# Weight slabs of 1 MB instead of 2 MB, and ten slots for gathered pairs instead of eight, in a two-block model kernel

## What is computed

```python
s1 = einsum("thd,hnd->thn", q1, k1)
s2 = einsum("thd,hnd->thn", q2, k2)
...
experts = (e1 * N_KEYS + e2)              # per token: 8 heads x 16 experts = 128
gates = softmax(sv)
hid = gelu(einsum("td,tkd->tk", xi, u_tab[ei]))
out = einsum("tk,tkd->td", gi * hid, v_tab[ei])
```

## Time and profile before

| what | value |
|---|---|
| time, median of 3 runs | 2146.59 us (2145.9 to 2158.28) |
| profiled execution | 2149.26 us |
| its span, as the profile counts it | 2147.5 us |
| PE busy | 1756.2 us (82%) |
| DVE busy | 1362.2 us (63%) |
| ACT busy | 828.3 us (39%) |
| POOL busy | 589.1 us (27%) |
| moved by DMA | 774.29 MB, 361 GB/s over the span |
| of that by POOL's queue (pairs) | 536.90 MB |
| of that by SP's queue (slabs and small inputs) | 236.04 MB |

### The profile page before, as it was taken

How to read it: one execution, slowest core, us unless ns; L and a number is a source line. 1 busy time by engine, 2 the same in 40 slices (tenths; PEclk the granted TensorE clock), 3 DMA queues, 4 the chain that set the end, 5 groups by cost and what they waited for, 6 DMA issues and landing times.

```text
span 2147.5 us, 21015 instructions
## 1 busy us (share of the span) xinstructions
PE 1756.2 (82%) x6868; PEld 1011.4 (47%) x6868; DVE 1362.2 (63%) x3461; ACT 828.3 (39%) x2114; POOL 589.1 (27%) x516
## 2 busy tenths in 40 slices
PE   7999988998978899977678887857788886778776
PEld 3448856583567464454225533722264362222222
DVE  3313336328866558757887686498888558785444
ACT  2323212523466336523344354233536414434333
POOL 0000000001222323533443343234433323444331
PEclk9999999899989999989988898878999897889999
DMA  8476847349799999999999999989999998999997
GB/s 349 185 277 237 302 187 274 125 180 392 322 419 414 415 374 417 403 421 392 406 394 417 419 399 382 419 328 414 420 419 419 376 419 333 395 415 420 420 419 306
DMA packets 108814, 774.29 MB, mean 361 GB/s; under 512 B 12192, under 2 KB 12704, under 8 KB 16544
## 3 DMA queue, kind: packets, MB, share of 16 engines
q0 software_dynamic: 73728, 536.90, 61.0%
q1 hardware_dynamic: 34976, 236.04, 27.8%
HBM read 771.85 MB, written 1.05 MB: 360 GB/s over the span
## 4 chain that ended last, share of the span: by engine, by line
PE 40%; DMA 32%; DVE 11%; issue 7%; ACT 6%; POOL 3%; SPq 0%; POOLq 0%; ACTq 0%; DVEq 0%
DMA arena<-in_peer_dram,eidx 16%; PE psum L1075 10%; PE psum L743 8%; PE psum L729 7%; DMA kv<-in_peer_dram,eidx 7%; DMA ring<-in_slabs_dram 6%; PE psum L924 6%; PE psum L942 3%; DMA ring<-in_peer_dram,eidx 3%; POOL arena L2107 2%; DVE arena L1956 2%; PE psum L774 1%; DVE x L1966 1%; ACT diag L1405 1%; ACT L1395 1%
## 5 line engine op out<-in xcount | busy, mean ns | idle before, releaser
L2107 POOL DMA_INDIRECT arena<-in_peer_dram,eidx x259 | 300.3, 1159 | 1035.7 <-DVE eidx L1827 490.9
L1075 PE MATMUL psum<-arena,diag 128*128 128x512 f32 x796 | 418.2, 659 | 144.5 <-ACT diag L1405 138.0
L1956 DVE CUSTOM_DVE_ANT_0 arena<-arena,osb 128x1024 f32<-128x1024 f32 x259 | 314.4, 1222 | 160.1 <-DMA arena<-in_peer_dram,eidx 159.8
L1395 ACT ACTIVATE wexp<-hid 128x1 f32<-128x1 f32 x512 | 103.2, 202 | 700.1 <-DVE hid L1956 698.7
L1075 PEld LDWEIGHTS psum<-arena,diag 128*128 128x128 f32 x796 | 156.3, 208 | 373.7 <-ACT diag L1405 210.8
L729 PE MATMUL psum<-ring,hT 128*128 128x512 f32 x560 | 260.4, 619 | 21.5 <-DMA ring<-in_slabs_dram 18.7
L1075 PE MATMUL psum<-kv,diag 128*128 128x512 f32 x400 | 211.6, 655 | 77.7 <-ACT diag L1405 77.7
L1075 PE MATMUL psum<-ring,diag 128*128 128x512 f32 x396 | 199.7, 630 | 42.7 <-ACT diag L1405 37.4
L2107 POOL DMA_INDIRECT kv<-in_peer_dram,eidx x131 | 151.6, 1157 | 295.9 <-PE psum L1075 207.5
L1956 DVE CUSTOM_DVE_ANT_0 kv<-kv,osb 128x1024 f32<-128x1024 f32 x131 | 160.1, 1223 | 73.5 <-DMA kv<-in_peer_dram,eidx 73.2
L743 PEld LDWEIGHTS psum<-hT,ring 128*128 128x128 f32 x1536 | 185.1, 201 | 31.7 <-DMA ring<-in_slabs_dram 17.0
(11 more groups left out here) (315 smaller groups left out, 1834.3 us busy)
## 6 DMA issues: line engine op xcount, KB each, us to landing
ring<-in_slabs_dram SPq DMA_DIRECT2D x206, 1024.0 KB, 9.0
ring<-in_slabs_dram SPq DMA_DIRECT2D x8, 768.0 KB, 6.1
arena<-in_peer_dram,eidx POOLq DMA_INDIRECT x259, 12.5
ring<-in_slabs_dram SPq DMA_DIRECT2D x8, 512.0 KB, 4.7
kv<-in_peer_dram,eidx POOLq DMA_INDIRECT x131, 12.8
kk<-in_keys_dram SPq DMA_DIRECT2D x2, 1024.0 KB, 9.4
ring<-in_peer_dram,eidx POOLq DMA_INDIRECT x122, 12.7
rowg<-in_rows_dram SPq DMA_DIRECT2D x3, 512.0 KB, 15.7
```

What stands on the lines that cost most here:

```text
L1075: ins = pe.matmul(bank(b), diags_of(n), pair(slot_of[n])[:, 1024 + 512 * h:1536 + 512 * h], start=(k == 0), stop=(k == 127))
L1395: act.activation(wn, hid[:, 128 * t + k:128 * t + k + 1], ACT.Gelu_apprx_tanh).then_inc(*up("gelu", n))
L1956: v.tensor_tensor_reduce(out=row, in0=row, in1=row_y[t], scale=1.0, scalar=0.0, op0=ALU.mult, op1=ALU.add, accum_out=hid[:, c:c + 1]).then ...
L2107: pool.indirect_dma_start(pair(i), None, tables, bass.IndirectOffsetOnAxis(ap=eidx[:, 128 * t + k:128 * t + k + 1], axis=0)).then_inc(sig. ...
```

## The change

All slabs become 1 MB (2048 columns). The ring has six places of 1 MB (`NRING`) until the first gather, and three (`NLATE`) after it; the three given up hold slots 7, 8 and 9 for pairs. One transfer fills a place. Per slab the halves are either the rows of a weight (`by_rows`, for `token_tile`) or its columns (`by_columns`, for `feature_tile`, mixers and branches); an FFN slab serves one feature group up, or two down. There are 220 slabs.

The masks `mdil` and `cdil`, the row gains `rows` and the table `cs` of cosines, needed by the first block alone, move into a new tile `early` of 2048 columns. It becomes slot 6 for pairs once attention of B1 is over. So there are ten slots: four in `arena`, two in `kv1`, one in `early`, three in the ring.

The planner gets one more cost: a step of a strand that takes a new slab is put back by `T_FRESH`, 0.5, while any strand holds a slab. `T_HEAD` goes from 40 to 50. `T_KEEP` and the other costs stay. At the start SP issues the identity before x.

```diff
-SLOT = 4096
-NSLOT = 3
 PAIR = 2048
+SLOT = 2048
+NRING, NLATE = 6, 3
...
-T_MB, T_SEEN, ..., T_HEAD = 2.5, 2.0, ..., 40
+T_MB, T_SEEN, ..., T_HEAD, T_FRESH = 2.5, 2.0, ..., 50, 0.5
...
-        rows = sb("rows", 384)
-        ring = sb("ring", NSLOT * SLOT)
+        ring = sb("ring", NRING * SLOT)
+        early = sb("early", PAIR)
-        cs = sb("cs", 2 * 128)
...
-            return kv1[...] if i < 6 else ring[:, two[0] % 3 * SLOT + PAIR * (i - 6):two[0] % 3 * SLOT + PAIR * (i - 5)]
+            if i < 7:
+                return early[:, :]
+            at_ = (less[0] + i - 7) % NRING
+            return ring[:, SLOT * at_:SLOT * at_ + SLOT]
...
         def place(n):
-            return n % 3 if n < two[0] else (two[0] + 1 + (n - two[0]) % 2) % 3
+            return n % NRING if n < less[0] else (less[0] + NRING - NLATE + (n - less[0]) % NLATE) % NRING
 
         def before(n):
-            return n - 3 if n < two[0] else n - 2
+            return n - NRING if n < less[0] else n - NLATE
...
-                        yield step_ready(e, s), wish(e, s, i), ("step", s)
+                        fresh = any(way[0] == "take" for way in ways[e][s][at_step[e, s]]) and any(holding[o] for o in STAGES)
+                        yield step_ready(e, s), wish(e, s, i) + (T_FRESH if fresh else 0.0), ("step", s)
...
                 if n == T_SHRINK:
                     load_slabs()
-                    two[0] = len(loaded)
-                    slots[6] = slots[7] = ("ring", 0)
+                    less[0] = len(loaded)
+                    slots.update({7 + i: ("ring", i) for i in range(NRING - NLATE)})
...
-                    w.wait_ge(sig.sem("slab%d" % place(n)), 32 * filled(n))
+                    w.wait_ge(sig.sem("slab%d" % place(n)), 16 * filled(n))
...
             def token_tile(s, b, hT_, name, *key, after=None):
-                weights, n = take(s)
-                wk = eight(weights)
                 for k in range(8):
+                    if k % 4 == 0:
+                        weights, n = take(s)
+                        wk = blocks_of(weights, 4, 512)
...
+                    if k == 3:
+                        ins.then_inc(*up("half", name, *key))
+                        consumed[n] = ("half", name, *key)
...
-                if n >= 3:
-                    w.wait_ge(*at(*consumed.get(before(n), ("ffn_down", 1, 5))))
-                for c in (slice(0, width // 2), slice(width // 2, width)):
-                    sp.dma_start(slot(n)[:, c], T["slabs"][i][:, c]).then_inc(sig.sem("slab%d" % place(n)), 16)
+                if n >= NRING:
+                    w.wait_ge(*at(*consumed.get(before(n), ("ffn_down", 1, 10))))
+                sp.dma_start(slot(n)[:, 0:width], T["slabs"][i][:, 0:width]).then_inc(sig.sem("slab%d" % place(n)), 16)
```

More of the change, by code:

```diff
@@ L478, in load_slabs @@
             def load_slabs():
-                while len(loaded) < 3 or used.get(before(len(loaded))) in seen:
+                while len(loaded) < NRING or used.get(before(len(loaded))) in seen:
                     n = len(loaded)
                     loaded.append(n)
-                    request("slab", n, seen[used[before(n)]] if n >= 3 else 0.0, 2.0)
+                    request("slab", n, seen[used[before(n)]] if n >= NRING else 0.0, 1.0)
             def transfer():
@@ L642, in gather @@
                     load_slabs()
-                    two[0] = len(loaded)
-                    slots[6] = slots[7] = ("ring", 0)
-                if n >= T_SHRINK and ("ring", 0) not in seen and used.get(two[0] - 3) in seen:
-                    seen["ring", 0] = seen[used[two[0] - 3]]
+                    less[0] = len(loaded)
+                    slots.update({7 + i: ("ring", i) for i in range(NRING - NLATE)})
+                for i in range(NRING - NLATE):
+                    if n >= T_SHRINK and ("ring", i) not in seen and used.get(less[0] - NRING + i) in seen:
+                        seen["ring", i] = seen[used[less[0] - NRING + i]]
                 free = [(seen[key], i) for i, key in slots.items() if key in seen]
@@ L850, in block @@
                         yield from turn_tile(s, mem3[:, u, :], b_[6:8], "turned_v", (sig.sem("l_m"), 16), "m%d" % u)
[L851 to L852 removed]
                     w.wait_ge(*at("turned_v", s, "m1", 1))
[L854 to L861 removed]
+                    for part in range(2):
+                        weights, n = take(s)
+                        wk = blocks_of(weights, 4, 512)
+                        for u in range(2):
+                            b = b_[2 + u]
+                            if part == 0:
+                                wait_bank(b)
+                            for k in range(4):
+                                ins = pe.matmul(bank(b), memT[:, 4 * part + k, 128 * u:128 * u + 128], wk[:, k, :],
+                                                start=(part == 0 and k == 0), stop=(part == 1 and k == 3))
+                            if part == 0 and u == 1:
+                                ins.then_inc(*up("half", "mem_kv"))
+                                consumed[n] = ("half", "mem_kv")
+                            if part == 1:
+                                ins.then_inc(*up("mem_kv", u))
+                                bank_free[b] = at("mem_out", u, 1)
+                            yield
                     consumed[n] = ("mem_kv", 1)
@@ L2099, in gather_program @@
                     w.wait_ge(*at("qp", "M00", 3))
-                elif i < 6:
+                elif i < 7:
                     w.wait_ge(*at("att_over", 1))
                 else:
-                    w.wait_ge(*at(*consumed.get(two[0] - 3, ("ffn_down", 1, 5))))
+                    w.wait_ge(*at(*consumed.get(less[0] - NRING + i - 7, ("ffn_down", 1, 10))))
                 w.wait_ge(*at("routed", l, t, k // 32))
@@ L2327, with by_rows, by_columns @@
-    wide(S_MEM, a["w_mem_kv"][0])
+        k, n = m.shape[0] // P, m.shape[1]
+        slabs[i, :, 0:k * n] = m.reshape(k, P, n).transpose(1, 0, 2).reshape(P, k * n)
+    def by_rows(i, m):
+        for part in range(2):
+            deep(i + part, m[512 * part:512 * part + 512])
+    def by_columns(i, m):
+        n = m.shape[1] // 2
+        for part in range(2):
+            deep(i + part, m[:, n * part:n * part + n])
+    for c in range(11):
+        by_rows(S_QKV + 2 * c, a["w_in"][0][:, 512 * c:512 * c + 512])
+        deep(S_DOWN + c, a["w_ffn_down"][0][256 * c:256 * c + 256])
```

202 lines of the change are left out of this document (96 added, 106 removed).

## The result

| | before | changed |
|---|---|---|
| median | 2146.24 us (4 runs, 2139.03 to 2158.28) | 2120.42 us (4 runs, 2115.70 to 2122.84) |
| profiled execution, span | 2147.5 us | 2121.0 us |

The ratio is 0.9871, with a 95% interval of 0.9823 to 0.9920: 1.3% faster, and 2121 us had been forecast. The number came out; a good part of the reasoning behind it did not.

What follows compares the result with a forecast made beforehand. PE was taken to bound the kernel up to the first gather at 491 us, then DMA standstill; 2149.3 - 2.5 - 5.8 - 22.2 + 5 = 2123.8, less 2.7: 2121 us, range 2098 to 2150.

Steps and rivals of the forecast that it cites:

- First slab: At the start, PE's first product waits for one 1 MB transfer instead of two; -2.5 us, bounds 0 to 4.05.
- Held slab: Near 328 us, PE's slab wait of 5.82 us goes, as M00's products end with its third small slab; -5.8 us.
- So the gather stage moves forward whole: The first gather and the stage behind it come 8.3 us earlier, with the same bytes and B1's progress.
- More waits: About 110 more slab waits on PE and on SP cost nothing; the bound kept was 11 us.
- rival E: Small slabs cost their waits (11 us) and the start gains nothing; 2141 us, chance 0.10.
- Shares of the two queues: With ten gathers in flight, slabs and pairs each wait by their own queue, so slabs keep their share; no cost.
- Pair slots: Ten slots for eight, net cover 2.5 or 5 us; all holes behind the first gather together -22.2 us.
- The table of M10 no longer late: At 1410 to 1420 us, DVE's new order reaches the table earlier and POOL's wait goes; -8.7 us.
- Given back by the long piece before pair 56: DVE runs M01's taps, log and scan in one piece of about 23 us, similarly before pair 311; +5 us.
- A: Slots are spent on the order, not cover; holes come back elsewhere, only the start is gained: 2138 us, chance 0.20.
- C: Long DVE pieces before pairs 56 and 311, and routings before 108 and 240, stop the DMA; 2176 us, chance 0.09.
- D: Three small slabs beside ten gathers get less traffic than before, 20 us on each of three strands; 2198 us, chance 0.03.

Runs made afterwards that it cites:

- e2: The changed kernel with the planner's cost for a new slab while another is held set to 0; 2122.9 us, ratio 0.9878.
- f2: The kernel before with both planner changes (hold of 50, new-slab cost 0.5), slabs still 2 MB, eight slots; 2146.7 us, ratio 0.9992.
- e1: The changed kernel with eight pair slots instead of ten and four 1 MB slab places once gathers run; 2118.4 us, ratio 0.9859.
- f4: The changed kernel with four 1 MB slab places once gathers run and nine pair slots; 2113.9 us, ratio 0.9847.
- g1: The changed kernel with five 1 MB slab places once gathers run and eight pair slots; 2104.6 us, ratio 0.9821.
- e4: The kernel before with a ninth pair slot alone, slabs still 2 MB; 2161.7 us, ratio 1.0054.
- f5: The changed kernel with two 1 MB slab places once gathers run and eleven pair slots; 2199.0 us, ratio 1.0260.
- e5: The changed kernel with the planner keeping six slots free instead of four before taking dots first; 2123.0 us, ratio 0.9902.
- f1: The kernel before with M00 held back behind B1 for 50 steps instead of 40, nothing else; 2150.6 us, ratio 1.0021.
- e3: The changed kernel with M00 held back behind B1 for 40 steps instead of 50; 2138.0 us, ratio 0.9939.

## Why the prediction was right, and where it was wrong

- First slab, -2.5 us: 3.06 us (13.12 to 10.06). Right.
- Held slab, -5.8 us: the wait is gone. Right, though "one strand's slab at a time" is only one of two things that remove it (e2, f2).
- "So the gather stage moves forward whole", by 8.3 us: wrong, 2.4 us in this profile and 3.8 us in the second. The prediction had named this as a sign against itself: it "is wrong if the first gather is not earlier by at least 5 us". PE was 12 us ahead at 346 us and lost over 9 of them by 433 us. The step left out PE's granted clock between 370 and 450 us, 0.87 before and 0.74 in both profiles of the changed kernel. In e1, in the same order at 0.85, the first gather is 11 us earlier. How much of the lower clock the new order brings and how much is chance is not shown; the 20 us from 370 have 1.00 before, and 0.55 to 0.66 in the changed kernel, e1, f4 and g1.
- More waits, 0 us: PE's waits for slabs behind the first gather became more and shorter, 15 of up to 6.5 us before, 38 of up to 3.4 us now, with the same sum (51.4 and 52.7 us). Costing them at nothing was right. Some tens of short slab waits, which were to speak for rival E, are thus there, without its price.
- Shares of the two queues: the strands were not starved with three places beside ten gathers, as the earlier trace rows had it. The Trainium skill ("DMA: Bandwidth & Descriptors", section "Queues, rings and completion order") has an engine go round-robin between its queues; the 13.4 us for a slab's megabyte beside 21.3 for a pair in the earlier trace rows agree with it, and no run here speaks against it. That a strand can be starved is seen with two places. Places weigh more in this than the number of gathers: from three places and ten slots to two and eleven the slab waits go from 52.7 to 131.8 us, but with four places they are 31.4 us with eight slots (e1) and 34.5 with nine (f4).
- Pair slots, -22.2 us: the size is near (47 to 20 us of idle DMA time by the stages, 54 to 31 by windows of 5 us), but the reason does not hold. This is the other step that failed. It gave 2.5 us of net cover per hole to the slots; e1, with none of these slots, has a gain of the same size, and e4, with one of them and large slabs, loses. The first hole closes to 1.3 us in e1 with eight slots. At the last routing the term came out in the changed kernel (3.8 us left, 5 forecast), though the other runs scatter there (7.6 to 11.4 us with eight, nine and eleven slots). The sum had no term for the grain at which a place comes free, nor for the number of places; "two places of 2 MB become three of 1 MB: in either case 2 MB are on their way" counted only what fits into the places. My reading, argued and not measured by itself: of 4 MB in two places, one place is held by PE and only 2 MB can be on their way; in four places of 1 MB it is 3 MB. PE's slab waits behind the first gather fit it: 51.4 us before (2 MB ahead), 52.7 changed (three places, also 2 MB), 31.4 in e1 and 34.5 in f4 (3 MB), 4.1 in g1 (4 MB), 131.8 in f5 (1 MB). By that reading the changed kernel is level with before in slab waits and gains by its slots and the finer grain together, e1 by its places alone.
- The table of M10 no longer late, -8.7 us: happened, and in every run with small slabs except e5. With large slabs the wait is there in all three, e4, f2 and f1 (22.7, 20.4 and 20.35 us). The profile puts that of f1 down to PE, but DVE writes the table at 1418.9 us and the gather follows it, as before:

```profile
1419.89 1.34 POOL L2107 DMA_INDIRECT kv<-in_peer_dram,eidx  x1 [20.35 <-PE psum L1075]
```

  e1 has it gone with eight slots, e4 keeps it with nine: it follows the planner's order, not the slots.
- Given back by the long piece before pair 56, +5 us: 0. The term counted ten pairs in flight, 23 to 25 us, and no slabs; slabs were 5.6 of the 12.6 MB that moved. Before pairs 240 and 311 there was nothing in this profile, and 4 us at the first in the second. The new hole is elsewhere, at `wf`, 4.8 us.

Of the rivals, A (only the start gained, 2138 us) was near e3 but not the change. C, slower through long pieces on DVE, did not come about at pair 56. D's price, strands that wait for slabs, is real, but at two places. Two errors, the start taken too large by 6 us (8.3 for 2.4) and what lies behind it too small by 7 (17.2 for 24), nearly cancelled, and so the sum of 25.5 us met the 26.5 us between the two spans. That the sum came so near is luck.

What stays open: small slabs with three places and only eight slots were not run, so it is not shown how much of the changed kernel's gain hangs on its two more slots; that small slabs gain by the places they leave ahead of PE fits the slab waits and the first hole, but no run changed that alone; an earlier load of `wf`, which would take the new hole, was not tried; and each setting changes the planner's order too, so a few us between two kernels (f4 and e1, 2114 and 2118) may be the order's own scatter.

## What to carry to other kernels

Where strands of matrix work and a stream of gathers share the DMA engines, divide the memory for weights into small places first: at the same 4 MB, four places of 1 MB beat two of 2 MB by 1.3%, and five places with eight slots were the fastest of all, 0.7% ahead of three places with ten. A stall that a buffer would cover is worth its length only if nothing else stands behind it, so test the buffer alone, and a new grain with the memory held equal. And when a planner makes the order, change one number at a time: a ninth slot alone made this kernel 0.5% slower.

## What the runs showed of the hardware

PE's order is the same up to the key scores of M00 in e1, e5, g1, f5, f4 and the changed kernel. Their first gathers came at 480.4, 481.2, 485.0, 486.1 and 487.2 us, and at 487.6 and 489.0 us in the two profiles of the changed kernel. The granted clock between 370 and 450 us was, in the same order, 0.85, 0.85, 0.79, 0.79, 0.74, 0.74 and 0.74. A gain of under 10 us ahead of a stage like this one can't be read from one profile.
